# High and low parts of each weight tile, interleaved element by element in one tile

## The reference, cut to what matters

```python
z = h @ w_in                                  # first block, 1024 x 7184
q = (ht @ peer_wq)
a = gelu(u @ h) * gate;  out = a @ vv         # all 16384 experts, peer_u and peer_v
mix = (...) @ w_out
up = x @ w_up;  down = act @ w_down           # second block
```

## Time and profile before

| what | value |
|---|---|
| runs | 1597.41 and 1597.86 us |
| span of the profiled execution, first to last instruction | 1595.2 us |
| what lies around the span, by the two runs | 2.2 and 2.7 us |
| TensorE busy | 1583.0 us (99%) |
| VectorE, ScalarE, GpSimd busy | 1071.3, 884.2, 885.8 us |
| HBM read | 274.73 MB, 173 GB/s over the span |

### The profile page before, as it was taken

One profiled execution on the slowest core, in us unless ns is written; L12 is line 12 of the kernel. 1 busy time (PEld: TensorE's weight loads), 2 busy tenths in 40 slices (PEclk: granted clock), 3 DMA queues, 4 the chain that ended last, 5 costly groups with the idle time before them and its releaser, 6 DMA issues.

```text
span 1595.2 us, 33476 instructions
## 1 busy us (share of the span) xinstructions
PE 1583.0 (99%) x12568; PEld 1493.5 (94%) x12568; DVE 1071.3 (67%) x1867; ACT 884.2 (55%) x1251; POOL 885.8 (56%) x413
## 2 busy tenths in 40 slices
PE   9999999999999999999999999999999999999998
PEld 8999899999999999998888888889999999999998
DVE  7998643779933777778888666776937383455521
ACT  6557766454454444444444445457676654666653
POOL 8786468868886000000000244457876689888886
PEclk9999999999999999999999999999999999999999
DMA  6565346555555555555555666666543356666653
GB/s 222 171 191 154 106 132 187 186 175 190 188 184 186 171 171 171 172 169 171 179 178 166 215 190 194 195 189 185 172 148 106 109 177 185 188 190 187 191 187 119
DMA packets 86218, 277.03 MB, mean 174 GB/s; under 512 B 11233, under 2 KB 18161, under 8 KB 86129
## 3 DMA queue, kind: packets, MB, share of 16 engines
q1 hardware_dynamic: 85712, 274.76, 54.9%
q0 software_dynamic: 272, 1.05, 0.2%
q10 hardware_dynamic: 144, 0.00, 0.0%
HBM read 274.73 MB, written 1.05 MB: 173 GB/s over the span
## 4 chain that ended last, share of the span: by engine, by line
PE 93%; issue 2%; DVE 2%; POOL 1%; ACT 1%; DMA 0%; SPq 0%; DVEq 0%; ACTq 0%; POOLq 0%
PE gemm L679 36%; PE gemm L982 22%; PE gemm L684 18%; PE aux L1268 4%; PE gemm L813 3%; PE aux L962 2%; POOL w_lo L462 1%; PE gemm L700 1%; PE gemm L725 1%; PE gemm L1268 1%; PE aux L932 0%; PE gemm L799 0%; ACT w_hi L1364 0%; PE gemm L706 0%; PE gemm L742 0%
## 5 line engine op out<-in xcount | busy, mean ns | idle before, releaser
L462 POOL TENSOR_TENSOR w_lo<-raw,w_hi 128x1024 fp32r<-128x1024 f32 (+1 forms) x330 | 791.7, 2407 | 294.7 <-ACT w_hi L1364 285.6
L1364 ACT ACTIVATE w_hi<-raw 128x1024 fp32r<-128x1024 f32 (+1 forms) x492 | 515.8, 1050 | 575.5 <-PE gemm L679 324.0
L679 PE MATMUL gemm<-h_lo,w_hi 128*128 128x256 f32 x2144 | 294.3, 279 | 0.0
L679 PE MATMUL gemm<-h_hi,w_hi 128*128 128x256 f32 x2096 | 293.3, 282 | 0.4 <-ACT w_hi L1364 0.3
L684 PE MATMUL gemm<-h_hi,w_lo 128*128 128x256 f32 x2096 | 288.6, 280 | 1.4 <-POOL w_lo L462 0.9
L679 PEld LDWEIGHTS gemm<-h_lo,w_hi 128*128 128x128 f32 x2144 | 268.9, 188 | 0.3 <-issue 0.2
L679 PEld LDWEIGHTS gemm<-h_hi,w_hi 128*128 128x128 f32 x2096 | 264.0, 188 | 3.3 <-issue 1.6
L462 DVE TENSOR_TENSOR w_lo<-raw,w_hi 128x1024 fp32r<-128x1024 f32 x162 | 196.6, 1222 | 104.3 <-ACT w_hi L1364 103.7
L684 PEld LDWEIGHTS gemm<-h_hi,w_lo 128*128 128x128 f32 x2096 | 262.8, 188 | 3.5 <-POOL w_lo L462 2.2
L982 PE MATMUL gemm<-w_hi,act_parts 128*128 128x512 f32 x1008 | 250.9, 391 | 0.4 <-ACT act_parts L1565 0.4
L982 PEld LDWEIGHTS gemm<-w_hi,act_parts 128*128 128x128 f32 x1008 | 188.0, 188 | 39.0 <-issue 0.5
(11 more groups left out here) (436 smaller groups left out, 2065.6 us busy)
## 6 DMA issues: line engine op xcount, KB each, us to landing
raw<-in_w_u SPq DMA_DIRECT2D x128, 512.0 KB, 3.6
raw<-in_w_ev SPq DMA_DIRECT2D x128, 512.0 KB, 3.7
raw<-in_w_up SPq DMA_DIRECT2D x48, 512.0 KB, 4.3
raw<-in_w_gate SPq DMA_DIRECT2D x24, 512.0 KB, 3.8
raw<-in_w_down SPq DMA_DIRECT2D x24, 512.0 KB, 4.0
raw<-in_w_conv_in SPq DMA_DIRECT2D x16, 512.0 KB, 4.6
raw<-in_w_peer_q SPq DMA_DIRECT2D x16, 512.0 KB, 3.5
raw<-in_w_branch SPq DMA_DIRECT2D x24, 288.0 KB, 2.9
```

The source lines that it names most:

```text
L462: eng.tensor_tensor(w_lo[v][:, 0:n], raw[c.raw][v][:, 0:n], w_hi[v][:, 0:n], ALU.subtract).then_inc(lo_ready[v], 1)
L679: mm = pe.matmul(out, w[:, k, :], act_part[:, k, :], start=(n == k == 0), stop=False)
L1364: act.activation(w_hi[v][:, 0:n], raw[c.raw][v][:, 0:n], ACT.Copy).then_inc(hi_ready[v], 1)
```

## The change

The four buffers become two, each of 128 partitions x 1024 x 2 float32r. The high part of tile v is the view of all elements with last index 0, the low part the view with last index 1. So element n of `w_hi[v]` and element n of `w_lo[v]` are neighbours, and each view has a step of two elements (8 bytes) from one element to the next. The total size is the same, 16 KiB in a partition, and every later buffer lies where it lay. No instruction is added, removed or moved, and no wait changes; what changes is the step of each operand that is `w_hi` or `w_lo`: written by ScalarE, read and written by GpSimd and VectorE, read by TensorE as the stationary or as the moving operand.

```diff
-        w_hi = [sb(f"w_hi{v}", [P, TILE], F32R) for v in range(2)]
-        w_lo = [sb(f"w_lo{v}", [P, TILE], F32R) for v in range(2)]
+        w_parts = [sb(f"w_parts{v}", [P, TILE, 2], F32R) for v in range(2)]
+        w_hi, w_lo = [[w_parts[v][:, :, part] for v in range(2)] for part in range(2)]
```

## The result

The changed kernel takes 2025.62 us (median; 2023.96 and 2027.29 shown) against 1597.63 us: 1.268 times, with a 95% interval of 1.2643 to 1.2717. The forecast was 1977 with a range to 2005. Direction and main mechanism came as forecast; the size came out 48.6 us higher, 20.6 us beyond the end of the range. The profiled execution of the changed kernel took 2027.29 us, with a span of 2025.2, so the span grew by 430.0 us.

What follows compares the result with a forecast made beforehand. TensorE was taken to bound the kernel. Doubled moving reads add 327.6 + 52.1 = 379.7 us to the 1595.2 us span, giving 1974.9, and 1977 us with the 2.4 us around it; range 1590 to 2005.

Steps and rivals of the forecast that it cites:

- What bounds it, and what doesn't change: Whole kernel: TensorE bounds it, busy 1583.0 of 1595.2 us at full clock; no instruction, wait or transfer added or moved.
- Weights as the moving operand: L982, L1010, L813: columns take double at step 8 bytes, adding 327.6 us over 1536 matmuls and 52.1 over 480.
- The 9.6 bytes per ns: TensorE's moving read: fastest walk through a partition seen, 512 x 4 bytes in 213.3 ns, taken as the limit.
- the span rule: TensorE's moving read: a step is free only while the span walked per ns stays at that of contiguous float32.
- Weights as the stationary operand: Weight loads of 8832 matmuls: 1024 bytes in 113 ns, 9.0 bytes per ns, so no cost taken.
- the cover: L679: the weight load is hidden with only some 3.6 ns to spare; every ns beyond costs 8.8 us.
- half of a doubling or the whole, as a rival: Slower weight load: half of the doubling about 2066 us, the whole 2567, without the moving term; chance 0.13.
- ScalarE, VectorE, GpSimd: Rounding and subtractions at the new step: no cost taken, operations staying at 1.06, 1.22 and 2.45 us.
- The rival by the 16-byte line: All operands: two hits in each 16-byte line keep full rate, L982 stays at 226.9 ns, 1598 us; chance 0.27.
- rival 1: Whole kernel: nothing gets slower, as two elements still share 16 bytes; 1598 us, chance 0.27.

Runs made afterwards that it cites:

- the runs of four: The change, but in the expert values the parts alternate every four elements (16 bytes) instead of single elements: 1688.30 us in a single run, against 1599.66.
- The narrow blocks: Not the kernel: matmul blocks, stationary operand contiguous or at step 2, under 192 and 128 moving columns; step 2 was 6.7 and 5.8 ns a load longer.
- the quiet blocks: Not the kernel: 48-matmul blocks, one access pattern each, no other engine working, then each helper alone; 512 moving float32r columns took 226.7 ns contiguous, 453.1 at step 2.

## Why the prediction was partly right, and what failed

**What bounds it, and what doesn't change.** Right: all of it is TensorE, the same work, full clock, L932 and L962 unchanged.

**Weights as the moving operand.** The mechanism chosen, doubling, was right, and the value too low. I doubled the 213.3 ns of columns and kept 13.6 ns beside them as they were; I even allowed that these might vanish, never that they would double. Measured is 2 x 226.7. The 9.6 bytes per ns were 2048 bytes over a column time worked out from the clock, which no row shows; over the 226.9 ns of the row they are 9.0 bytes per ns, and 4096 bytes at that rate give 453.8 ns. For L982 the term was 327.6 and came to 348.1 us; for L813 52.1 and 53.9. The reasoning behind it was wrong in a way that happened to give the same factor, which was luck: it is not bytes of span per ns, as the runs of four show, but 16-byte lines that are used in part. I had even read one witness for the span rule, the gate matmuls at a step of 4 bytes. They touch 16 lines in 30.6 ns, 1.9 ns a line, so they fit both rules; a row that fits two rules shouldn't have been the choice between them.

**Weights as the stationary operand: the step that failed.** "I take no cost" came out as 28.0 us, 3.2 ns each over 8832 matmuls. The text itself called the cover thin: 3.6 ns, and 8.8 us for every ns beyond. The narrow blocks show a load longer by 6 to 7 ns, which at that price gives 21 to 30 us. So the account fits that the cover took the first part and the rest came through, though no block shows it at 256 columns. What failed is to put the load at nothing on the ground of a rate of bytes, and to allow otherwise only for half of a doubling or the whole, as a rival. A few ns of load are a cost of the same change as the moving read, and add to it: 5 ns on each of 8832 matmuls would have put 44 us on the forecast's upper end.

The moving terms and the load together make the difference to the profiled execution: 1977 + 20.5 + 1.8 + 28.0 = 2027.3 us, which must come out so, as 28.0 is the remainder.

**ScalarE, VectorE, GpSimd.** Right in effect. ScalarE's 91 ns, VectorE's 6 and GpSimd's 36 are hidden, as GpSimd had 0.39 us of room. By the Trainium skill, "Vector Engine (DVE) Microarchitecture Reference", section 5.2, an estimate for VectorE at a step of two words is some 1.9 us. Measured are 1228 ns in the kernel and 1220 in the quiet blocks, so it doesn't hold there. At four words the quiet block took 1999 ns, near that estimate: the loss is there, one step further out.

**The rival by the 16-byte line.** L982 moved from 226.9 to 453.5 ns, so it fell. The Trainium skill, "SBUF — State Buffer", section Specifications (TRN2), asks for two hits in a line for full bandwidth. By these runs that holds nearly for ScalarE, VectorE and TensorE's weight load (5%, none, and 6 ns of some 113 at two hits; about double or 64% more at one). It doesn't hold for the moving operand: two hits in a line cost double already in both types (453.1 and 451.7 ns), while four hits cost little (231.3 ns in float32r, 225.8 in bfloat16).

**Range.** It ran from rival 1 to the forecast's upper end and ended 20.6 us short. The moving terms were 22.3 us too small and the load 28.0; either error alone would have left the time inside 2005, and the range had no room for both.

## What to carry to other kernels

Count the 16-byte lines of what TensorE reads as its moving operand: 1.77 ns a line here, and in float32r never more than about 0.9 ns a column. If two parts must share a tile, keep each in halves or alternate them in runs of 16 aligned bytes (226.9 and 232.1 ns), never element by element (453.5). And where one operation that is hidden by a few ns occurs thousands of times, give its few ns a term in the sum, beside the main cost rather than as its rival.

## What the runs showed of the hardware

- A moving float32r operand is held by its reads even when contiguous: 226.7 ns for 512 columns, against 216.3 for bfloat16.
- Its cost stops growing at about 0.88 ns a column: 453.1, 450.0, 461.3 and 431.0 ns at steps 2, 3, 4 and 8, while bfloat16 goes on to 900.0 at step 8. No run says why.
- The stationary operand behaves otherwise: about 6 ns for step 2 where the load is the limit, none under 256 columns in the blocks (120.0 ns), and 233.3 ns a matmul in place of 120.0 at step 4.
- In the quiet blocks the granted clock fell without a gap in TensorE's work: it was 1.00 until 313 us and 0.50, the 1.2 GHz level, from there to 408 us. It fell 4 us into the bfloat16 block at step 8, whose matmuls lie 900 ns apart before the fall and after it; so that row of the table doesn't hang on the level. The matmuls of 128 columns behind it, which waited for their loads, ran at 0.50 throughout, and the clock came back 3 us into the first block of 256 columns. These blocks are not used above for that reason.
